# Forgetting-attention logits in three float32r products of split queries and keys, in place of float32 products

## What is computed

```python
h = rmsnorm(x, norm1_g)
z = h @ w_in + b_in                                  # 1024 -> 5648 columns
mq, mk, mv, mo, mi, mf, fq, fk, fv, ff, gm, gf = split(z)
hm = mlstm_chunkwise(silu(conv(mq, mk)), mv, mi, log_sigmoid(mf))      # 4 heads of 128
# forgetting attention: 8 heads of 64, query blocks of 128, causal
logits = einsum("td,sd->ts", q, k) * 64 ** -0.5 + (cum[t] - cum[s])    # cum = cumsum(log_sigmoid(ff))
y_f = softmax(mask(logits)) @ v
mix = sigmoid(gm) * (y_m @ w_br_mlstm) + sigmoid(gf) * (y_f @ w_br_fox)
x = x + mix @ w_out
x = x + swiglu(rmsnorm(x, norm2_g), w_gate, w_up, w_down)
out = rmsnorm(x, norm_f_g)
```

## Time and profile before

| | |
|---|---|
| median of 3 runs | 783.08 us (783.08 to 783.25) |
| profiled execution | 783.5 us |
| its span, first to last instruction | 781.7 us |
| TensorE (PE) busy | 98% of the span, 3919 matmul records |
| VectorE (DVE) busy | 47% |
| ScalarE (ACT) busy | 33% |
| GpSimd (POOL) busy | 3% |
| chain that ended last, by engine | PE 91%, DVE 3%, ACT 2% |
| memory traffic | 75.6 MB, mean 97 GB/s |
| mean granted TensorE clock | 0.997 of full speed |

### The profile page before, as it was taken

One profiled execution on the slowest core, in us unless ns is written; L12 is line 12 of the kernel. 1 busy time (PEld: TensorE's weight loads), 2 busy tenths in 40 slices (PEclk: granted clock), 3 DMA queues, 4 the chain that ended last, 5 costly groups with the idle time before them and its releaser, 6 DMA issues.

```text
span 781.7 us, 9654 instructions
## 1 busy us (share of the span) xinstructions
PE 766.8 (98%) x3919; PEld 630.8 (81%) x3919; DVE 370.2 (47%) x565; ACT 254.5 (33%) x422; POOL 24.8 (3%) x46
## 2 busy tenths in 40 slices
PE   6999999999899999999999999999999999999996
PEld 6988888878576788888889888888888888888885
DVE  4679623157878525244355443433444445123224
ACT  6444311244455332232243333222323323213111
POOL 4000000012200000000000000000000000000000
PEclk9999999999999999999999999999999999999999
DMA  8433324211111135332311423322333323422302
GB/s 232 121 108 112 123 94 157 62 51 51 54 56 55 37 100 188 108 107 82 134 54 55 130 87 107 108 84 79 108 109 108 108 68 116 127 72 86 125 1 107
DMA packets 61916, 75.64 MB, mean 97 GB/s; under 512 B 3680, under 2 KB 49840, under 8 KB 61872
## 3 DMA queue, kind: packets, MB, share of 16 engines
q1 hardware_dynamic: 61872, 75.02, 30.1%
HBM read 72.92 MB, written 2.10 MB: 96 GB/s over the span
## 4 chain that ended last, share of the span: by engine, by line
PE 91%; DVE 3%; ACT 2%; issue 2%; DMA 1%; POOL 1%; SPq 0%; POOLq 0%; DVEq 0%; ACTq 0%
PE bank L1179 29%; PE bank L1180 28%; PE bank L1181 28%; PE bank L1420 1%; PE bank L1382 1%; DMA stage<-in_w_in 1%; PE bank L1403 1%; ACT decay L575 1%; POOL head_rs L449 1%; DVE decay L936 0%; PE bank L1389 0%; DVE head_ms L925 0%; PE bank L1192 0%; DVE hT_lo L732 0%; ACT ymT_hi L557 0%
## 5 line engine op out<-in xcount | busy, mean ns | idle before, releaser
L1179 PE MATMUL bank<-hT_hi,w_hi 128*128 128x512 f32 (+1 forms) x680 | 259.6, 382 | 2.5 <-DVE hT_lo L732 2.5
L747 DVE TENSOR_TENSOR w_lo<-stage,w_hi 128x1024 fp32r<-128x1024 f32 x125 | 152.4, 1223 | 226.0 <-ACT w_hi L489 217.5
L1180 PE MATMUL bank<-hT_lo,w_hi 128*128 128x512 f32 (+1 forms) x680 | 257.0, 378 | 0.0
L1181 PE MATMUL bank<-hT_hi,w_lo 128*128 128x512 f32 (+1 forms) x680 | 256.9, 378 | 0.0
L489 ACT ACTIVATE w_hi<-stage 128x1024 fp32r<-128x1024 f32 x127 | 133.4, 1053 | 128.0 <-PE bank L1181 121.9
L1179 PEld LDWEIGHTS bank<-hT_hi,w_hi 128*128 128x128 f32 x680 | 128.7, 189 | 25.8 <-POOL w_lo L433 2.7
L1181 PEld LDWEIGHTS bank<-hT_hi,w_lo 128*128 128x128 f32 x680 | 128.7, 189 | 23.6
L1180 PEld LDWEIGHTS bank<-hT_lo,w_hi 128*128 128x128 f32 x680 | 128.8, 189 | 22.4
L1179 PE MATMUL bank<-w_hi,aT_hi 128*128 128x512 f32 x176 | 68.5, 389 | 0.0
L1180 PE MATMUL bank<-w_lo,aT_hi 128*128 128x512 f32 x176 | 68.5, 389 | 0.0
L1181 PE MATMUL bank<-w_hi,aT_lo 128*128 128x512 f32 x176 | 68.5, 389 | 0.0
(11 more groups left out here) (180 smaller groups left out, 738.3 us busy)
## 6 DMA issues: line engine op xcount, KB each, us to landing
stage<-in_w_in SPq DMA_DIRECT2D x21, 1024.0 KB, 5.2
stage<-in_w_gate SPq DMA_DIRECT2D x11, 1024.0 KB, 5.3
stage<-in_w_up SPq DMA_DIRECT2D x11, 1024.0 KB, 5.4
stage<-in_w_down SPq DMA_DIRECT2D x22, 512.0 KB, 4.3
stage<-in_w_out SPq DMA_DIRECT2D x4, 1024.0 KB, 4.9
x_nat<-in_x SPq DMA_DIRECT2D x4, 512.0 KB, 5.4
stage<-in_w_br_mlstm SPq DMA_DIRECT2D x4, 512.0 KB, 3.5
stage<-in_w_br_fox SPq DMA_DIRECT2D x4, 512.0 KB, 4.5
```

The costliest lines, as they stand in the source:

```text
L747: dve.tensor_tensor(ring(w_lo, g), staged(g), ring(w_hi, g).bitcast(F32), ALU.subtract).then_inc(lo_split, 1)
L1179: pe.matmul(o, a_hi, b_hi, start=first, stop=False)
L1180: pe.matmul(o, a_hi, b_lo, start=False, stop=False)
L1181: return pe.matmul(o, a_lo, b_hi, start=False, stop=last)
```

## The change

`q_f` and `k_f` become four tiles each, one for each pair of heads. For each pair of heads hp there are four new float32r tiles: `qf_hi`, `kf_hi` (ScalarE copies) and `qf_lo`, `kf_lo` (VectorE subtractions, written over `q_f` and `k_f`). The high halves of pairs 1 to 3 lie where `q_m` and `k_m` of the mLSTM were, so they wait for its last scores (`s_m`). `fox_logits` makes three float32r products for each head in place of the float32 one, and waits at every fourth step for the low halves of its pair (`fqk_lo_ready`).

- Pair 0 of the heads: split before the mLSTM heads on ScalarE, and after `weigh_scores(0)` on VectorE.
- Pairs 1, 2, 3: ScalarE copies both after `fox_softmax(v + 2)` of v = 0, 4, 8. VectorE subtracts the queries at the end of step v = 0, 4, 8 and the keys at the end of step v = 1, 5, 9, behind a granule split where there is one.

```diff
@@ ScalarE, before the mLSTM heads
+            act.wait_ge(fq_ready, 1)
+            act.activation(qf_hi[0][:, :], q_f[0][:, :], ACT.Copy).then_inc(fqk_hi_ready, 1)
+            act.wait_ge(fk_ready, 1)
+            act.activation(kf_hi[0][:, :], k_f[0][:, :], ACT.Copy).then_inc(fqk_hi_ready, 1)
             act.wait_ge(m_step, 1)
...
+            def split_fox_hi(hp, keys):
+                act.wait_ge(s_m, ROWS * H_M)
+                act.wait_ge(fk_ready if keys else fq_ready, hp + 1)
+                act.activation((kf_hi if keys else qf_hi)[hp][:, :], (k_f if keys else q_f)[hp][:, :],
+                               ACT.Copy).then_inc(fqk_hi_ready, 1)
@@ ScalarE, fox loop, end of step v
                 if v + 2 < FOX_PAIRS:
                     fox_softmax(v + 2)
+                if v % ROWS == 0 and v // ROWS + 1 < KB:
+                    split_fox_hi(v // ROWS + 1, False)
+                    split_fox_hi(v // ROWS + 1, True)
@@ VectorE
+            def split_fox_lo(hp, keys):
+                dve.wait_ge(fqk_hi_ready, 2 * hp + keys + 1)
+                dve.tensor_tensor((kf_lo if keys else qf_lo)[hp][:, :], (k_f if keys else q_f)[hp][:, :],
+                                  (kf_hi if keys else qf_hi)[hp][:, :].bitcast(F32), ALU.subtract).then_inc(fqk_lo_ready, 1)
+
             for h in range(H_M):
                 mask_stabiliser(h)
                 weigh_scores(h)
+                if h == 0:
+                    split_fox_lo(0, 0)
+                    split_fox_lo(0, 1)
@@ VectorE, fox loop, end of step v
                 if v in SPLIT_AT:
                     split_lo(G_BR + AHEAD + SPLIT_AT.index(v))
+                if v % ROWS == 0 and v // ROWS + 1 < KB:
+                    split_fox_lo(v // ROWS + 1, 0)
+                if v % ROWS == 1 and v // ROWS + 1 < KB:
+                    split_fox_lo(v // ROWS + 1, 1)
@@ TensorE, fox_logits
                 hp, q = fox_pair(v)
+                if v % ROWS == 0:
+                    pe.wait_ge(fqk_lo_ready, 2 * hp + 2)
                 if v == 0:
-                    pe.wait_ge(fq_ready, KB)
-                    pe.wait_ge(fk_ready, KB)
                     pe.wait_ge(rows_low_half, 3)
...
+                rows = slice(q * P, (q + 1) * P)
                 for h2, head in enumerate(heads):
-                    pe.matmul(banks[h2][:, 0:n], q_f[head, hp, q * P:(q + 1) * P], k_f[head, hp, 0:n],
-                              start=True, stop=False)
+                    pe.matmul(banks[h2][:, 0:n], qf_hi[hp][head, rows], kf_hi[hp][head, 0:n], start=True, stop=False)
+                for h2, head in enumerate(heads):
+                    pe.matmul(banks[h2][:, 0:n], qf_hi[hp][head, rows], kf_lo[hp][head, 0:n], start=False, stop=False)
+                for h2, head in enumerate(heads):
+                    pe.matmul(banks[h2][:, 0:n], qf_lo[hp][head, rows], kf_hi[hp][head, 0:n], start=False, stop=False)
```

More of the change, by code:

```diff
@@ L182, in block_kernel @@
         k_m = at("k_m", [P, H_M, SEQ], F32, R + 8 * K)
-        q_f = at("q_f", [P, KB, SEQ], F32, R + 16 * K)
-        k_f = at("k_f", [P, KB, SEQ], F32, R + 24 * K)
+        q_f = [at(f"q_f{i}", [P, SEQ], F32, R + (16 + 2 * i) * K) for i in range(KB)]
+        k_f = [at(f"k_f{i}", [P, SEQ], F32, R + (24 + 2 * i) * K) for i in range(KB)]
+        qf_lo = [at(f"qf_lo{i}", [P, SEQ], F32R, R + (16 + 2 * i) * K) for i in range(KB)]
+        kf_lo = [at(f"kf_lo{i}", [P, SEQ], F32R, R + (24 + 2 * i) * K) for i in range(KB)]
+        qf_hi = [at(f"qf_hi{i}", [P, SEQ], F32R, R + (66 if i == 0 else 4 * i) * K) for i in range(KB)]
+        kf_hi = [at(f"kf_hi{i}", [P, SEQ], F32R, R + (68 if i == 0 else 4 * i + 2) * K) for i in range(KB)]
         o_gate = at("o_gate", [P, KB, SEQ], F32, R + 32 * K)
@@ L277, in block_kernel @@
         logits, fox_max, fox_exp, fox_norm, fox_T, fox_pv = (sem(n) for n in ("logits", "fox_max", "fox_exp", "fox_norm", "fox_T", "fox_pv"))
+        fqk_hi_ready, fqk_lo_ready = sem("fqk_hi_ready"), sem("fqk_lo_ready")
         fox_PT = [sem("fox_PT_high"), sem("fox_PT_low")]
@@ L547, in _ @@
                     act.wait_ge(used, g + 1)
-                    act.activation(k_f[:, b, :], psum[fqk_bank(KB + b)][:, :], ACT.Identity,
+                    act.activation(k_f[b][:, :], psum[fqk_bank(KB + b)][:, :], ACT.Identity,
                                    bias=vec[:, V_FQK + KB + b:V_FQK + KB + b + 1]).then_inc(fk_ready, 1)
+            act.wait_ge(fq_ready, 1)
+            act.activation(qf_hi[0][:, :], q_f[0][:, :], ACT.Copy).then_inc(fqk_hi_ready, 1)
+            act.wait_ge(fk_ready, 1)
+            act.activation(kf_hi[0][:, :], k_f[0][:, :], ACT.Copy).then_inc(fqk_hi_ready, 1)
             act.wait_ge(m_step, 1)
@@ L895, in _ @@
                     dve.wait_ge(used, g + 1)
-                    dve.tensor_scalar(q_f[:, b, :], psum[fqk_bank(b)][:, :], vec[:, V_FQK + b:V_FQK + b + 1],
+                    dve.tensor_scalar(q_f[b][:, :], psum[fqk_bank(b)][:, :], vec[:, V_FQK + b:V_FQK + b + 1],
                                       DH_F ** -0.5, ALU.add, ALU.mult).then_inc(fq_ready, 1)
```

## The result

The changed kernel takes **790.52 us** (median of 5 runs, 789.81 to 792.78) against 783.25 us (5 runs, 783.08 to 784.72) for the kernel before on the same chip: a ratio of 1.0096, 95% interval 1.0083 to 1.0109, or 7.3 us slower. 789.8 us was forecast.

A forecast was written before the change was run, and what follows sets the result against it. TensorE, busy 98% of the span, was taken as the bound. +3.5 + 1.05 + 1.8 - 3 x 0.41, plus 1.5 for the clock, made +6.7: 790.2 profiled, 0.4 lower against the median, 789.8 us; range 785.4 to 791.7.

The forecast's parts named there:

- the side that had 0.91: Whole kernel: chance 0.91 that it becomes slower by more than about 0.2% (1.6 us).
- TensorE's own part: Fox logits: three float32r products replacing two float32 passes save 0.41 us per head pair, 1.64 us for all sixteen pairs.
- The rule on loads: Logits products: weight loads overlap only across differing row groups; one more open load per pair would cost 1.7 us.
- Head pair 0: Splits before the mLSTM heads: price 0, covered by VectorE's 2.54 us wait before o_gate; uncovered, up to 2.1 us.
- Head pair 1: Fox steps 0 to 2: VectorE waits for ScalarE's copy, kf_lo comes late, TensorE starts pair 4's logits +3.5 us later.
- Head pairs 2 and 3: Logits of pairs 8 and 12: late key halves delay TensorE by a further +1.05 and +1.8 us.
- The clock: Fox loop, after TensorE's new 2.7 us wait: 3.4 us at half speed, costing 1.5 us (bounds 0 and 1.7).
- The sum: Whole kernel: waits less products' savings, +5.1 to 5.2, plus 1.5 for lowered clock speed, make +6.7 us.
- That the clock stays up: Fox loop: the same waits but no fall of the clock, 788.3 us; chance 0.30.
- VectorE catching up: Fox loop: only the first wait is real, and in part; +2.3 us, 785.4 us; chance 0.10.
- Rival 4: Logits: loads lie open or heads do not overlap, +1.9, 791.7 us; or a second clock fall, about same; chance 0.10.
- Rival 3: Fox loop: the halves are ready before TensorE asks, so the kernel is faster, 781.5 us; chance 0.05.

The follow-up runs named there:

- the last kernel: The changed kernel with every copy and subtraction placed where its own engine stood idle, against the kernel before: 782.14 us against 783.58, ratio 0.9984.

## Why the prediction was right

The forecast was 789.8 us and the measured median 790.52, within the range and on the side that had 0.91. Point by point:

- **TensorE's own part: mis-sized.** The step that failed is "per pair 3 x 0.014 - 2 x 0.004 = 0.03 us more", taken from products of 512 columns and carried to 128. The starts above are 0.23 us apart at 512 columns but 0.11 at 128 (233.07, 233.18, 233.29), where the prediction's reckoning gives 0.054 + 0.014 = 0.07. So three passes of 128 columns take about 0.33 us, and two float32 passes, at the 0.11 of the prediction, 0.22. The blocks save 0.13, 0.09, 0.05 and lose 0.14 us at 512, 384, 256 and 128 columns, 0.13 per head pair and not 0.41. The transposes before them give back 0.03 in the step looked at (245.69 - 245.14 = 0.55 us from transposes to logits before, 244.56 - 244.04 = 0.52 in the last kernel). If every step gives as much, it is some 1.0 us in all by the traces; by the medians it is 0.7, and not 1.64.
- **The rule on loads.** The Trainium skill, "TensorE: Matmul & The Clock Gate", section "The mechanism", was set aside. The trace does not agree with it at 512 columns: the step of 0.23 us, of which the prediction's reckoning gives 0.216 to the columns, leaves no room for an open load of 107 ns, as the section "LDWEIGHTS (loading the stationary operand)" gives it for 128 columns. The step of 0.11 us at 128 columns is near that load time, but that the load sets it is not shown: the sixteen transposes that start at 245.14 us before, whose loads also have 128 columns and 64 rows, take 0.55 us, 0.034 each, or 0.07 for every two if two run beside each other.
- **Head pair 0: right,** price 0 (measured -0.6 us, interval reaching 0). The rest of the wait at o_gate was 1.3 us and not 0.5: only VectorE's 1.2 us came off it, ScalarE's 0.9 did not.
- **Head pair 1: right.** +3.5 was forecast; from the row maxima of step 2 to the logits of step 4 it was 213.67 - 209.44 = 4.23 us and became 218.38 - 210.75 = 7.63, +3.40. qf_lo waited 1.35 us (1.4 forecast), high(1) was 2.04 late (2.05), TensorE waited 2.53 (2.7).
- **Head pairs 2 and 3: about right.** Waits of 0.9 and 1.6 us were forecast; they are 0.66 and 1.39. From the logits of step 8 to those of step 12 it is 14.61 us and was 12.96, 1.65 more; 1.8 - 0.41 = 1.4 was forecast. From step 4 to step 8 the low clock is mixed in; with products in the wait, where it stays up, it is 16.21 us and was 15.49, 0.7 more, and 1.05 - 0.41 = 0.6 was forecast.
- **The clock: right that it falls, its length unsure.** 3.4 us low and 1.5 us of cost were assumed. Two kernels were low for 3.4 us (splits and wait, with the same wait of 2.5 us; key half before the granule, with one of 1.4), the profiled run of the change for 6.8, of which 5.8 with TensorE at work, some 2.9 us. That run is the one of 792.78 us. The cost by the medians is 1.5 to 1.7 us.
- **The sum.** 5.2 for the waits and 1.5 for the clock made 6.7; measured 7.3. The forecast had taken off 3 x 0.41 us for the last three head pairs' products; with 3 x 0.13 for their blocks it would have been 0.8 higher, 7.5, and what head pair 0 saves is lost in the first wait, as it said.
- **Rivals.** That the clock stays up (0.30) is refuted by its row; VectorE catching up (0.10) by the second and third wait. Rival 4 (0.10) fails in both its parts: blocks of 512 columns became shorter, and from 227 to 270 us the clock is 1.00. Rival 3, that the halves are there in time (0.05), named the right condition, "a VectorE queue that did not wait for the copy", and what it was worth: 781.5 by my numbers, 782.14 in the kernel that meets it.
- **What I had not seen:** that removing TensorE's wait alone would leave 4.9 us. The chain that I followed to kf_lo had a second end at the gate's tanh. It ended at 214.73 us before, and TensorE's gate products behind it started at 215.01, so VectorE's lateness had only 0.3 us in hand there.

## What to carry to other kernels

When splitting work moves onto two in-order queues, place each piece where its own engine is idle in the trace, with its input made a step earlier, and do not put the second engine directly behind the first: the same copies and subtractions cost nothing that could be measured apart, 4.9 us tied together, and gained 1.4 us when spread. A wait that the profile names is the last of several; look for the next one within its length before you count on removing it. Do not carry a pass's price from 512 columns to 128: here it was 0.11 us and not 0.07.

## What was not expected of the hardware

- A float32r pass over half the rows, two heads at once, takes 0.11 us from start to start at 128 columns; at 256, 384 and 512 it takes 0.12, 0.18 and 0.23.
- A subtraction of 512 columns on GpSimd (1.29 us in the row above) and VectorE's in-place divisions beside it hold each other up: the divisions take 1.11 and 1.21 us in place of 0.49, and other subtractions on GpSimd in that kernel 1.46 and 1.72. So it is with VectorE's operations of two inputs: 1.74 us in place of 0.69 in that kernel, and a granule's low half 1.96 in place of 1.22 where the subtractions stand in the change's places. The kernel before has one such place, a division of 128 columns that starts at 199.86 us beside GpSimd's square and takes 1.10 us, where the next takes 0.29.
- The length of a wait does not tell whether the clock falls. In and just ahead of the fox loop it fell after every wait of 2.3 to 2.5 us, for 3.4 or for 6.8 us; near the start of the last kernel two waits of 2.3 us left it at 1.00 (from 0 to 24 us). After one of 1.4 us, the first for a half with the key half before the granule, it fell too; after the third wait of the same kernel and of the changed one, also 1.4 us, it stayed at 1.00, as it did in the loop after waits of at most 1.0 us (2.8 us in three) for the gate's tanh.
